# Two weights per normalised row, and row scales worked out with tokens on partitions

## What is computed

```
def rmsnorm(x, g):
    y = x * rsqrt(mean(x * x, axis=-1) + 1e-6)
    return y * g

h = rmsnorm(x, g_mix) * (1 + scale1) + shift1          # h1
proj = h @ w_in                                        # dilated and neighbourhood attention
...
x = x + gate1 * (merged @ w_out)                       # out
h2 = rmsnorm(x, g_ffn) * (1 + scale2) + shift2         # h2
u = depthwise_conv_seq(h2 @ w_up, conv_w, conv_b)      # up
x = x + gate2 * ((gelu(u_gate) * u_val) @ w_down)      # down
x = rmsnorm(x, g_final)                                # gfinal
for l in range(2):                                     # latents x and context ctx
    x, ctx = hybrid_layer(...)   # norm, three attention branches, merge, out
                                 # q = rms_norm(qc, q_norm) @ w_uq, kv = rms_norm(kvc, kv_norm) @ w_ukv
return rms_norm(x, final_norm)                         # final
```

## Time and profile before

| | |
|---|---|
| median of 3 runs | 4202.91 us (4201.59 to 4203.57) |
| profiled execution | 4200.46 us, its span 4198.70 us |
| TensorE matmul busy | 3807.2 us, 91% of the span |
| weight loads (PEld) busy | 2896.7 us, 69% |
| VectorE busy | 2163.3 us, 52% |
| ScalarE busy | 1392.2 us, 33% |
| mean granted TensorE clock | 0.959 |
| chain that ended last | TensorE 76%, VectorE 12%, ScalarE 4%, VectorE's queue 4%, transfers 1% |

### The profile page before, as it was taken

How to read it: one execution, slowest core, us unless ns; L and a number is a source line. 1 busy time by engine, 2 the same in 40 slices (tenths; PEclk the granted TensorE clock), 3 DMA queues, 4 the chain that set the end, 5 groups by cost and what they waited for, 6 DMA issues and landing times.

```text
span 4198.7 us, 55667 instructions
## 1 busy us (share of the span) xinstructions
PE 3807.2 (91%) x20685; PEld 2896.7 (69%) x20685; DVE 2163.3 (52%) x3446; ACT 1392.2 (33%) x2473; POOL 0.2 (0%) x4
## 2 busy tenths in 40 slices
PE   5988989999799999999798998988999999789998
PEld 3655768877567787777586666865667777566666
DVE  3555345553555525777524555245553777535544
ACT  2433233322233313444312443122332444314432
POOL 0000000000000000000000000000000000000000
PEclk8998999999899999999899999998999999899999
DMA  6443325542101121111121101211112111121122
GB/s 235 138 112 98 90 80 164 167 135 80 36 25 30 31 60 46 35 35 40 31 60 31 31 21 41 65 40 39 33 39 80 50 45 40 51 65 36 36 60 71
DMA packets 491824, 273.23 MB, mean 65 GB/s; under 512 B 40153, under 2 KB 477365, under 8 KB 491678
## 3 DMA queue, kind: packets, MB, share of 16 engines
q1 hardware_dynamic: 470770, 249.98, 21.1%
q10 hardware_dynamic: 20908, 21.26, 1.6%
HBM read 268.99 MB, written 10.32 MB: 67 GB/s over the span
## 4 chain that ended last, share of the span: by engine, by line
PE 76%; DVE 12%; ACT 4%; DVEq 4%; issue 3%; DMA 1%; ACTq 1%; SPq 0%; PEldq 0%; PEld 0%
PE ps L553 72%; PE ps L936 3%; PE ps L885 2%; ACT probs L775 1%; ACT w_high L539 1%; DVE w_low L549 1%; DVE y_low L2243 1%; DVE row_max L796 1%; DVE neg_max L800 1%; DVEq L797 1%; DVE probs L1340 1%; DVEq L1222 1%; DVE probs L1829 1%; DVE probs L1846 1%; DMA w_raw<-in_w_in 0%
## 5 line engine op out<-in xcount | busy, mean ns | idle before, releaser
L553 PE MATMUL ps<-h_high,w_high 128*128 128x512 f32 (+2 forms) x3448 | 1299.6, 377 | 137.2 <-DVE h_low L1838 44.6
L553 PE MATMUL ps<-h_low,w_high 128*128 128x512 f32 (+2 forms) x3448 | 1262.8, 366 | 0.0
L553 PE MATMUL ps<-h_high,w_low 128*128 128x512 f32 (+2 forms) x3448 | 1260.3, 366 | 0.0
L553 PEld LDWEIGHTS ps<-h_high,w_high 128*128 128x128 f32 (+1 forms) x3448 | 662.4, 192 | 304.8 <-issue 143.3
L549 DVE TENSOR_TENSOR w_low<-w_raw,w_high 128x1024 fp32r<-128x1024 f32 x374 | 449.0, 1201 | 638.0 <-ACT w_high L539 614.0
L553 PEld LDWEIGHTS ps<-h_high,w_low 128*128 128x128 f32 (+1 forms) x3448 | 662.2, 192 | 106.3
L553 PEld LDWEIGHTS ps<-h_low,w_high 128*128 128x128 f32 (+1 forms) x3448 | 664.3, 193 | 94.3 <-issue 2.4
L539 ACT ACTIVATE w_high<-w_raw 128x1024 fp32r<-128x1024 f32 x374 | 387.9, 1039 | 695.8 <-PE ps L553 526.2
L775 ACT ACTIVATE probs<-ps,neg_max 128x768 f32<-128x768 f32 (+2 forms) x368 | 289.5, 789 | 643.0 <-DVE neg_max L800 440.2
L553 PE MATMUL ps<-probsT,v 128*128 128x512 f32 (+4 forms) x736 | 287.7, 561 | 10.3 <-DVE probsT L993 8.8
L553 PE MATMUL ps<-k_high,q_high 64*128 64x256 f32 (+4 forms) x784 | 186.0, 397 | 117.1 <-ACT probs L775 58.7
(11 more groups left out here) (204 smaller groups left out, 4016.7 us busy)
## 6 DMA issues: line engine op xcount, KB each, us to landing
w_raw<-in_w_in SPq DMA_DIRECT2D x436, 256.0 KB, 3.1
y_and_merged<-in_w_mod SPq DMA_DIRECT2D x96, 256.0 KB, 3.2
w_raw<-in_w_branch SPq DMA_DIRECT2D x96, 256.0 KB, 3.0
w_raw<-in_w_up SPq DMA_DIRECT2D x88, 256.0 KB, 4.3
y_and_merged<-in_w_ada SPq DMA_DIRECT2D x64, 256.0 KB, 3.3
w_raw<-in_w_out SPq DMA_DIRECT2D x48, 256.0 KB, 3.0
w_raw<-in_w_down SPq DMA_DIRECT2D x44, 256.0 KB, 2.9
y_and_merged<-in_w_ada SPq DMA_DIRECT2D x4, 2048.0 KB, 20.6
```

The source lines that it names most:

```text
L553: return nc.tensor.matmul(*a, **kw)
```

## The change

- Two weights are used for each normalised row: the new `pe_rows_two` takes, as each row of h comes out, the three matmuls of the first weight and then those of the second (three rows behind, where there is no context in the first weight), in `dil`, `up` and `pre`. For this both weights are split within the norm.
- The sums of squares are taken with the squares as weights, 128 tokens at a time, against two columns of ones (`pe_sums`): the result has tokens on partitions, 4 or 6 columns. Root and reciprocal work on these (`RT`), and `pe_spread` brings the factors back to all partitions by a product of the broadcast column and the identity, into banks 4 and 5, from where the scaling reads them. The low-rank latents are done in the same way (`LT2`).
- In the three `out` stages ScalarE squares each finished row, and TensorE adds its sums behind a later projection: rows 0 to 5 are summed in `out`, 6 and 7 in the norm (h2, layer 1, final).
- gfinal squares rows as `down` finishes them (`down_ev`), and layer 0 as gfinal finishes them (`fin`); ScalarE skips the wait of the fence behind `down` and gfinal, TensorE behind gfinal.

The core of the diff ("..." marks what is left out):

```
+        def pe_rows_two(pe, s, per, pairs, ready):
+            base = s.base["h"]
+            k = [base % 2, (base + 1) % 2]
+            lag = 0 if len(pairs[0]) > 1 else 3
+            def trio(j, kc, lo, n, ps):
+                both = [(WR[:, k[j], kc, :], HR[:, kc, lo:lo + n]), (WR[:, k[j], kc, :], HL[:, kc, lo:lo + n]), (WL[:, k[j], kc, :], HR[:, kc, lo:lo + n])]
...
+            pe.wait_ge(s_low, base + 2)
+            for kc in range(NK):
+                pe.wait_ge(S[ready], s.base[ready] - 8 + kc + 1)
+                for lo, n, ps in pairs[0]:
+                    last = trio(0, kc, lo, n, ps)
+                if kc == NK - 1:
+                    last.then_inc(s_h, 1)
+                if kc >= lag:
+                    last = trio(1, kc - lag, *pairs[1][0])
+            for kc in range(NK - lag, NK):
+                last = trio(1, kc, *pairs[1][0])
+            for lo, n, ps in pairs[1][1:]:
+                for kc in range(NK):
+                    last = trio(1, kc, lo, n, ps)
+            last.then_inc(s_h, 1)
...
+        def pe_sums(b, kc, ctx):
+            for tt in range(tiles_of(ctx)):
+                last = mm(bank(b, 2, 2 * tt), SQ[:, kc % 2, 128 * tt:128 * tt + 128], ones[:, 0:2], start=kc + tt == 0, stop=kc == NK - 1,
+                          skip_group_check=True)
+            last.then_inc(S["square_mm"], 1)
+        def pe_spread(dst, rows, ctx):
+            for tt in range(tiles_of(ctx)):
+                ps = bank(dst, 128, 128 * tt) if tt < 4 else bank(dst + 1, 128, 128 * (tt - 4))
+                last = mm(ps, rows[:, tt:tt + 1].to_broadcast([128, 128]), ident[:, :], start=True, stop=True, skip_group_check=True)
+            return last
         def pe_norm(pe, s):
...
-            for kc in range(s["nk"]):
+            for kc in range(6 if done_in_out(s) else 0, NK):
                 pe.wait_ge(S["square"], s.base["square"] + kc + 1)
-                for x, lo, n, a, b in norm_source(s, kc):
-                    last = mm(bank(0 if lo == 0 else 1, n), ones[:, :], SQ[:, kc % 2, lo:lo + n], start=kc == 0, stop=kc == s["nk"] - 1)
-                last.then_inc(S["square_mm"], 1)
+                pe_sums(norm_bank(s), kc, s["ctx"])
+            pe.wait_ge(S["rinv"], s.base["rinv"] + 1)
+            pe_spread(4, RT, s["ctx"]).then_inc(S["spread"], 1)
...
         def act_norm(act, s):
...
+                if s["what"] == "gfinal":
+                    act.wait_ge(S["down_ev"], s.base["down_ev"] - 8 + kc + 1)
+                if s["what"] == "layer" and s["l"] == 0:
+                    act.wait_ge(S["fin"], s.base["fin"] - 8 + kc + 1)
+                act_row(act, s, kc)
+                if kc == (7 if done_in_out(s) else 3) and s["what"] in ("h2", "layer"):
+                    act_high(act, Stage("first", h_end=None).at(s.base), 0, 0, 1)
...
-                last = act.activation(RS[:, lo:lo + n], bank(0 if lo == 0 else 1, n), ACT.Sqrt, scale=1.0 / s["size"], bias=EPSB[:, :])
+            act.activation(RT[:, 0:nt], sums[:, :, 0], ACT.Sqrt, scale=1.0 / s["size"], bias=EPSB[:, :]).then_inc(S["rstd"], 1)
+            if s["what"] == "h1":
+                act_high(act, Stage("first", h_end=None).at(s.base), 0, 0, 1)
...
-            v.reciprocal(RS[:, 0:n0], RS[:, 0:n0])
+            v.reciprocal(RT[:, 0:nt], RT[:, 0:nt]).then_inc(S["rinv"], 1)
             if s["what"] == "h1":
-                dve_low(dve, Stage("first", h_end=None).at(s.base), 0, 0, 0)
+                for j in range(2):
+                    dve_low(dve, Stage("first", h_end=None).at(s.base), 0, 0, j)
+            dve.wait_ge(S["spread"], s.base["spread"] + 1)
...
-                    last = v.scalar_tensor_tensor(out=dst, in0=x, scalar=a, in1=RS[:, lo:lo + n], op0=ALU.mult, op1=ALU.mult)
+                    last = v.scalar_tensor_tensor(out=dst, in0=x, scalar=a, in1=bank(4 if lo == 0 else 5, n), op0=ALU.mult, op1=ALU.mult)
+                if s["what"] == "gfinal":
+                    last.then_inc(S["fin"], 1)
...
         # out, TensorE
+                    if not isinstance(t, int):
+                        pe.wait_ge(S["square"], cnt(s, "square", t, 2, u - 1))
+                        out_sums(u, t)
...
+                for u in range(2):
+                    body(1, u, 2 + u)
+                    pe.wait_ge(S["square"], s.base["square"] + u + 1)
+                    pe_sums(6, u, s["ctx"])
+                with pe.Fori(2, 4) as t:
...
         # pre, TensorE
+                pe_rows_two(pe, s, 0, (tgroups(0, s["cq"]), tgroups(2, s["cq"])), "low_row")
...
+                    if j == 4:
+                        pe_latent_spread(pe, s, 0, s.base["lat_ri"])
...
         # fence
+            if me == "act" and (s.kind == "down" or s["what"] == "gfinal"):
+                return
+            if me == "pe" and s["what"] == "gfinal":
                 return
```

More of the change, by code:

```diff
@@ L157, in plan @@
         if k == "norm":
-            add(s, square=s["nk"], square_mm=s["nk"], rstd=1)
+            add(s, square=s["nk"], square_mm=s["nk"], rstd=1, rinv=1, spread=1)
+            if s["what"] == "gfinal":
+                add(s, fin=8)
             if s["rows"]:
@@ L577, in pe_split @@
                 pass
+        def pe_rows_two(pe, s, per, pairs, ready):
+            base = s.base["h"]
+            k = [base % 2, (base + 1) % 2]
+            lag = 0 if len(pairs[0]) > 1 else 3
+            assert per is not None
+            def trio(j, kc, lo, n, ps):
+                both = [(WR[:, k[j], kc, :], HR[:, kc, lo:lo + n]), (WR[:, k[j], kc, :], HL[:, kc, lo:lo + n]), (WL[:, k[j], kc, :], HR[:, kc, lo:lo + n])]
+                for e, (a, b) in enumerate(both):
+                    last = mm(ps, a, b, start=kc == 0 and e == 0, stop=kc == NK - 1 and e == 2, skip_group_check=True)
+                return last
[14 more added lines that the diff above has]
+            last.then_inc(s_h, 1)
         def few(steps, n):
@@ L1155, in act_proj_qk @@
             per = s["nh"]
-            if first:
+            if first and name != "dil":
                 act_high(act, s, t, per, 1)
@@ L1868, in pe_latent, with pe_latent_spread @@
                 pe.wait_ge(S["lat_sq"], s.base["lat_sq"] + kc + 1)
[L1869 to L1870 removed]
+                for tt in range(latent_tiles(s, g)):
+                    last = mm(bank(5 + 2 * g, 2, 256 + 2 * tt), LSQ[:, kc, 128 * tt:128 * tt + 128], ones[:, 0:2], start=kc == LROWS[g][0] and tt == 0,
+                              stop=kc == LROWS[g][-1], skip_group_check=True)
             last.then_inc(S["lat_ss"], 1)
+        def pe_latent_spread(pe, s, g, base):
+            pe.wait_ge(S["lat_ri"], base + g + 1)
+            pe_spread(4 + 2 * g, LT2[:, g, :], g == 1 or s["cq"]).then_inc(S["lat_sp"], 1)
         def act_square(act, s, j):
@@ L1967, in pe_stage, with out_sums @@
                     pe_rows(pe, s)
+                def out_sums(u, t):
+                    for tt in range(tiles_of(s["ctx"])):
+                        last = mm(bank(6, 2, 2 * tt), SQ[:, u, 128 * tt:128 * tt + 128], ones[:, 0:2], start=False, stop=False,
+                                  skip_group_check=True)
+                    last.then_inc(S["square_mm"], 1)
                 def body(t, u, i):
```

108 lines of the change are left out of this document (68 added, 40 removed).

## The result

The changed kernel takes 4169.57 us (median of 4 runs, 4165.80 to 4173.89) against 4202.25 us for the kernel before on the same chip (4199.58 to 4203.57): 0.9924 of it, 95% interval 0.9911 to 0.9936. It is faster, by 32.7 us where 55.9 were forecast. The profiled execution took 4173.89 us, its span 4172.1 us, the mean granted clock 0.956 (before: 0.959).

What follows compares the result with a forecast made beforehand. TensorE, busy in most of the span, was taken as the bound, its idle time as winnable. Eight stretch terms summed to 55.9 us, from 4200.46 to 4144.6, plus 2.45 for the median: 4147 us, range 4128 to 4172.

Steps and rivals of the forecast that it cites:

- The forecast of faster, and the range: Whole kernel: 45 to 65 us won, chance 0.62; range 4128 to 4172 us; faster at all, chance 0.93.
- out and h2: Sums moved into `out` cost 5.8 us; earlier first scaling wins 9.2 and earlier third weight 3.3: 6.7 us won.
- out and the second layer norm: Moved sums cost 8.7 us; earlier first scaling wins 13.2 and earlier third weight 7.0: together 11.5 us won.
- pre, second layer: `pre` of layer 1: spreading costs 1.2 us, k/v come earlier and at a higher clock: 2.8 us won.
- out and final: Moved sums cost 5.8 us in the last `out`; the final norm's first scaling comes at 4174.0, not 4182.95: 3.1 won.
- gfinal and the first layer norm, to its first scaling: Early squares, narrow sums and short reciprocals bring layer 0's first scaling from 1080.87 to 1068.7: 12.2 us won.
- The first layer's rows: Layer 0, two weights per row: third weight starts 23.3 us after the first scaling instead of 32.5: 9.2 us won.
- pre, first layer: `pre` of layer 0: latent sums and spreading about even; second latent group brings k/v forward by 1.9 us.
- h1: First norm and next head pair: third weight 9.0 us earlier, limited by the weights' transfer; 8.5 us won, bounds 5.5 and 14.
- The rival "slower": Clock falls to 0.50 wherever the 328 narrow products stand, costing 76 us more: 4223 us; chance 0.05.
- The rival "rows stay at 1.2 GHz": Clock stays low while normalised rows come, about 20 us lost: 4167 us; chance 0.17 with the transfer bound of h1.
- PSUM as a source of the scaling: Scaling reads its factor from PSUM at no extra cost; bounds 0.05 us less or more an instruction, 3 us overall.

Runs made afterwards that it cites:

- Experiment 5: Changed kernel with the two weights of the first projection used one after the other instead of in step on each row; 4177.01 us, 0.9947 of the kernel before.
- experiment 6: Changed kernel with all squares and narrow sums of h2, layer 1 and the final norm put back behind `out`; 4193.94 us, 0.9985 of the kernel before.
- experiment 8: Changed kernel with the write of the NA rows moved into the second head pair of `dil`; 4172.69 us, 0.9936 of the kernel before.
- experiment 10: Changed kernel with the write of the NA rows issued ahead of h1's squares; 4163.07 us, 0.9919 of the kernel before.
- experiment 1: Changed kernel with sum products widened from 2 columns of ones to 128 (h1, gfinal) or 80 (layer 0); 4156.34 us, 0.9900 of the kernel before.
- experiment 2: Changed kernel with sum products of h1, gfinal and layer 0 all widened to 128 columns of ones; 4151.31 us, 0.9885 of the kernel before.
- experiment 7: Kernel before the change with the write of the NA rows moved into the second head pair of `dil`; 4207.73 us, 1.0018 of the kernel before.

## Why the prediction was right in part

*The forecast of faster, and the range.* The time lies inside the range, at its upper end; the likeliest value was 23 us too good. The forecast proper, 45 to 65 us won, was missed with 32.7. The range held because it reached over a rival whose mechanism did not happen, and that is luck.

*out and h2* (6.7 forecast): right in both terms. `out` pays 0.95 us a row, the norm behind it wins 11.1 us up to 691.

*out and the second layer norm* (11.5), *pre, second layer* (2.8), *out and final* (3.1): right. From 2806 to 2925 20.7 us were won of 21.5, at the end 6.6 of 6.0.

*gfinal and the first layer norm, to its first scaling* (12.2): wrong, 4.6 us were lost in the trace of after, and between 0.7 us won and 1.5 us lost in experiments 5, 6, 8 and 10. The step that failed is the price of a narrow product, 0.233 us, taken at clock 1.00 from sixteen loads in the modulation and used for places where the clock is another. I had kept 0.47 as a bound, and the measured price here is 0.43. gfinal's sums were put at 7.5 us and took 13.65 (9.99 to 10.83 in those four); layer 0's at 11.2 us and took 20.64; the spreading at 0.98 and 1.47 took 2.08 and 2.93. That is 6.2 + 9.4 + 2.6 = 18.2 us, which covers the 16.8 us missing. Experiments 1 and 2 are the proof: the same products with more columns bring back 17.8 us between 1005 and 1106 against the trace of after, and still 12.4 against the quickest of the others, experiment 8.

*The first layer's rows* (9.2): right, 8.8 us. The third weight starts 23.75 us behind the first scaling (forecast 23.3, before 32.55), though the clock was at 0.50 until 1088.0, 8 us behind it. Experiment 5 shows that 4.6 us of it are the second weight in step.

*pre, first layer* (1.9): wrong, 4.1 us were lost behind the third weight's start. The sums and the spreading were rightly sized: 2.74 us for the second group's sums where 2.8 were forecast, 1.50 us for each spreading. What the sum had at nothing is the clock behind them. It was granted 0.50 in four spells here, in one before (1155.1 to 1158.5), and the products around those spells took longer:

```profile
1149.24 5.78 PE L557 MATMUL ps<-y_and_merged 128*96 128x512 f32 x12 [0.26 <-issue]
...
1158.63 4.37 PE L557 MATMUL ps<-y_and_merged 128*64 128x512 f32 x8 [2.28 <-DVE y_and_merged L1989]
...
1167.06 4.30 PE L557 MATMUL ps<-y_and_merged 128*128 128x128 f32 x24 [2.96 <-DVE qT L1260]
```

The first of them had been, in the kernel before,

```profile
1159.28 4.08 PE L553 MATMUL ps<-y_and_merged 128*96 128x512 f32 x12 [0.26 <-issue]
```

and the other two took 2.79 and 2.94 us: together 4.6 us. The remaining spell, 3.4 us of dense products from 1125.6 on, costs another 1.7, an estimate (half its length). That makes 6.3 us, against 6.0 missing. What brings the clock down there was not tried.

*h1* (8.5, bounds 5.5 to 14): 2.6 at 119 us, 0.5 at 565, below the lower bound. Two steps failed. The sums were put at 0.7 us more for the low level and took 3.65 us more than the wide ones, so the first scaling came 17.3 us behind the first square's start where it had come after 16.4. And the transfer: I had the second weight behind the write land near 99; ScalarE got it at 105.95, 24.5 us behind the write's issue at 81.42. The 24.4 us read off the kernel before held again, and my allowance of 2 us and the earlier issue did not. Experiment 8 against 7 gives h1's worth with the write away, 6.7 us. A further 3.4 us went at the start of `na`, where the weights of the next pair came later (SP's issue of eight loads at 237.99 took 16.9 us instead of 14.0); the runs differ here by 2 to 4 us, and its cause was not tried.

*The rival "slower".* It named the right mechanism, a clock of 0.50 where narrow products stand, with the wrong reach. Of the 328 products, 145 ran so in the trace of after (h1 36, gfinal and layer 0 90, both with their spreading, and 19 of the last row's sums and the spreading at h2 and layer 1), some 0.2 us too dear each, 29 us; the 183 others, mostly between dense products, did not. I had taken the mechanism for all or nothing. My argument against it, 1.00 granted over sixteen loads, was a row of 1.86 us behind other work and no evidence for 13.7 us of such products.

*The rival "rows stay at 1.2 GHz"* (4167) is close to the time by accident: at h2, layer 0 and layer 1 the clock did rise within the rows. The Trainium skill (page "TensorE: Matmul & The Clock Gate", section "Part 1: The HAM clock gate") names two levels, 1.2 GHz when TensorE was idle and 2.4 GHz when it was busy. Taken by the profile's busy time, that rule would give gfinal's sums, 13.69 us busy of 13.70, the higher level, and by an estimate from the terms above the change would win 18 us more. The row says 0.50, and the measurement decides.

*PSUM as a source of the scaling* cost nothing, as taken from the earlier trace rows: 0.747 us an instruction, the same as from SBUF.

## What to carry to other kernels

Price a short matmul by where it stands: the same two-column fp32 product cost 0.24 us among dense products and 0.43 us in a run of its own, so move such work between dense products, or give it more columns: 128 took no longer here than 2. Where a stage is won in front of a large transfer, look first at when the next weights can land; moving the transfer moves the stall, and each queue that its issue can block counts. When a change has several parts, set the gain by stretch against the forecast by stretch: the total alone would have hidden misses of 8, 17 and 6 us. Cut such a table at the same work in both kernels, and look at more than one trace: a cut at the third weight's splitting would have hidden that 8.8 us were won in layer 0's rows and 4 us lost behind them, and gfinal's stretch alone ranges over 5.3 us among kernels that are alike in it.

## What the runs showed of the hardware

- A run of 13.8 us (h1), 13.7 us (gfinal) and 20.6 us (layer 0) of two-column fp32 products without a gap was granted 0.50 throughout; with clock 1.00 at its start (gfinal in experiment 8) such a run kept it for 4.0 of its 9.99 us and then was granted 0.50. 128 columns at the same places were granted 0.71, 1.00 and 0.88, and 80 columns at layer 0 0.56. With fp32r, 128 columns were granted 0.50.
- A two-column fp32 product costs 0.23 to 0.24 us at clock 1.00 and 0.43 us at 0.50, one of 128 columns 0.237 us at 1.00. In fp32r two columns cost 0.12 to 0.15 us and 0.24 us.
- The issue of a 3.8 MB write on ScalarE's queue took 0.67 us in `dil` (78.86, 35.6 us behind the issue of a 4 MB write on the same queue) and 4.81 and 6.15 us when it was issued 5.3 us behind it (48.55 after 43.22, 49.27 after 43.95).
